# Row sums as four wide products, and token copies shared by alternate banks and awaited by halves

## The reference

```python
# first stack: DEPTH = 2, 16 heads of 64, D_FF = 2816
for layer in range(2):
    h = h + 0.5 * swiglu(rmsnorm(h, g1[layer]), ...)      # ffn0, ffn2
    hn = rmsnorm(h, gm[layer])
    h = h + (mixer_a(hn, ...) if layer == 0 else mixer_b(hn, ...))   # attention a, attention b
    h = h + 0.5 * swiglu(rmsnorm(h, g2[layer]), ...)      # ffn1, ffn3
    if layer == 0: shared = shared_kv(h, kv_norm, kv_w)   # keys and values of mixer_b
x = rmsnorm(h, final_norm)
# second stack: cs = silu(c), one vector of 1024
mod = cs @ ada_w[l] + ada_b[l]         # 6 rows of 1024 a layer, and 2 rows for the shared K/V
h = x * (1 + sc_m) + sh_m
y = rwkv7_time_mix(h) if l == 0 else fox_layer(h, kv)
x = layer_norm(ALPHA * x + (1 + gt_m) * y)
y = hier_moe(x * (1 + sc_f) + sh_f)    # 32 experts, top 2
x = layer_norm(ALPHA * x + (1 + gt_f) * y)
```

## Time and profile before

| | |
|---|---|
| median of three runs | 2657.39 us (2653.95 to 2661.37) |
| span of the profiled execution | 2656.2 us (its whole time isn't recorded beside it) |
| mean granted TensorE clock | 0.961 of 2.4 GHz |
| TensorE waits for expert gate weights | 59.9 us in 55 waits |
| TensorE waits for expert up weights | 19.0 us in 28 waits |
| row products of `mod_sums` | 224 passes in seven groups, 6.9 us a group |
| HBM read | 687.85 MB, 259 GB/s over the span |

### The profile page before, as it was taken

How to read it: one execution, slowest core, us unless ns; L and a number is a source line. 1 busy time by engine, 2 the same in 40 slices (tenths; PEclk the granted TensorE clock), 3 DMA queues, 4 the chain that set the end, 5 groups by cost and what they waited for, 6 DMA issues and landing times. The chain is left out here.

```text
span 2656.2 us, 40656 instructions
## 1 busy us (share of the span) xinstructions
PE 2450.2 (92%) x16214; PEld 1713.2 (64%) x16214; DVE 1291.0 (49%) x2016; ACT 736.4 (28%) x1086; POOL 157.2 (6%) x250
## 2 busy tenths in 40 slices
PE   8999999999998899999998999899888899999896
PEld 7998789989997799944885343333367653343332
DVE  7864468746875576445564321222266552222223
ACT  4334443334334433312221111111033521111111
POOL 1100001000110010020240000000000000000000
PEclk9999889999999899989998999999998999999998
DMA  8865238754873175433004899999953159999996
GB/s 336 309 236 181 74 123 311 277 191 175 316 277 127 64 271 212 166 130 131 33 4 153 360 423 423 424 423 424 422 191 133 48 215 423 423 423 424 423 424 280
DMA packets 110172, 690.77 MB, mean 260 GB/s; under 512 B 15760, under 2 KB 17104, under 8 KB 35168
## 3 DMA queue, kind: packets, MB, share of 16 engines
q1 hardware_dynamic: 88720, 618.10, 59.0%
q0 software_dynamic: 20320, 70.85, 7.2%
q10 hardware_dynamic: 1008, 0.06, 0.0%
HBM read 687.85 MB, written 1.11 MB: 259 GB/s over the span
## 5 line engine op out<-in xcount | busy, mean ns | idle before, releaser
L737 PE MATMUL bank<-ring,B 128*64 128x512 f32 (+1 forms) x1728 | 548.1, 597 | 59.9 <-DMA ring<-in_moe_wgate 59.9
L2045 DVE TENSOR_TENSOR ring_r<-ring,B_r 128x2048 fp32r<-128x2048 f32 x184 | 417.8, 2289 | 273.1 <-ACT B_r L1592 272.9
L737 PE MATMUL bank<-B_r 128*128 128x512 f32 (+1 forms) x1992 | 534.0, 353 | 13.8 <-DVE B_r L2382 6.0
L1592 ACT ACTIVATE B_r<-ring 128x2048 fp32r<-128x2048 f32 x184 | 347.0, 1909 | 293.7 <-PE bank L737 290.6
L737 PEld LDWEIGHTS bank<-B_r 128*128 128x128 f32 x1992 | 344.9, 193 | 111.3 <-issue 50.7
L737 PE MATMUL bank<-xt_r,B_r 128*128 128x256 f32 x1408 | 399.8, 284 | 5.4 <-DVE xt_r L2026 2.5
L737 PE MATMUL bank<-xt_r,ring_r 128*128 128x256 f32 x1408 | 398.4, 283 | 0.0
L737 PEld LDWEIGHTS bank<-ring,B 128*64 128x64 f32 (+1 forms) x1728 | 183.9, 143 | 325.1 <-issue 315.4
L737 PE MATMUL bank<-B 64*64 64x64 f32 (+7 forms) x2528 | 244.8, 289 | 38.8 <-DMA rows<-in_moe_wup 19.0
L737 PEld LDWEIGHTS bank<-xt_r,B_r 128*128 128x128 f32 x1408 | 269.9, 192 | 8.0 <-issue 5.2
L737 PEld LDWEIGHTS bank<-xt_r,ring_r 128*128 128x128 f32 x1408 | 269.9, 192 | 0.0
(11 more groups left out here) (361 smaller groups left out, 2895.8 us busy)
## 6 DMA issues: line engine op xcount, KB each, us to landing
ring<-in_moe_wgate SPq DMA_DIRECT2D x128, 1024.0 KB, 23.4
rows<-in_moe_wup SPq DMA_DIRECT2D x64, 1024.0 KB, 24.8
wks<-in_moe_wdown SPq DMA_DIRECT2D x64, 1024.0 KB, 23.1
ring<-in_ffn_w_gate SPq DMA_DIRECT2D x44, 1024.0 KB, 4.9
ring<-in_ffn_w_up SPq DMA_DIRECT2D x44, 1024.0 KB, 7.4
ring<-in_ffn_w_down SPq DMA_DIRECT2D x44, 1024.0 KB, 7.4
wks<-in_ada_w POOLq DMA_DIRECT2D x72, 512.0 KB, 6.1
ring<-in_moe_wup SPq DMA_DIRECT2D x32, 1024.0 KB, 22.7
```

Source lines behind the costliest of these rows:

```text
L737: ins = pe.matmul(out, lhsT, rhs, start=start, stop=stop, skip_group_check=True)
L1592: act.activation(hi, ring[:, slot, :], ACT.Copy).then_inc(sp_hi, 1)
L2045: dve.tensor_tensor(ring_r[:, slot, :], ring[:, slot, :], f32(hi), ALU.subtract).then_inc(sp_lo, 1)
```

## The change

1. `mod_sums`: four products with the column of ones as the stationary operand and 512 columns of the accumulator as the moving one. Product j writes row 32j of bank 7. ScalarE copies 97 rows of 512 columns, and the DMA takes every 32nd.
2. Fillers (`FILLED`) ahead of the transposes of mix_a, kv, mix_b (3), mix_r (6), ffn1 and ffn3 (4), in bank 4.
3. ScalarE copies banks 0 and 2 of a set of transposes, VectorE banks 1 and 3. The consumer on TensorE waits for the first two banks, and for the last two only where it needs them (`copied`).
4. In the first slab of an ffn both gate products come before both up products, and the wait for ScalarE's copy of the row moves behind the first gate product.
5. VectorE's split of the first projection unit at mix_a, kv and mix_b is cut in two halves, one before and one after the norm; at ffn1 and ffn3 the up split moves behind the low parts; at ffn2 VectorE copies tokens before it splits, and ScalarE copies them between its two splits.

```diff
+COPIED = {"qkv_a": "mix_a", "wo_a": "o_a", "kv_b": "kv", "q_b": "mix_b", "wo_b": "o_b", "kv_f": "kv_f", "wo_f": "o_f"}
+FILLED = {"mix_a": 3, "kv": 3, "mix_b": 3, "mix_r": 6, "ffn1": 4, "ffn3": 4}
...
-                for c in range(MODW // P):
-                    mm(bank[7][:, c:c + 1], mod_acc[r % 2].rearrange("p (m c) -> p c m", m=P)[:, c, :], cst("upto", TB, SEQ)[:, 0, SEQ - 1:SEQ],
-                       signal=mod_pe if c == MODW // P - 1 else None)
+                for j in range(MODW // BANK):
+                    mm(bank[7][32 * j:32 * j + 1, :], cst("upto", TB, SEQ)[:, 0, SEQ - 1:SEQ], mod_acc[r % 2][:, j * BANK:(j + 1) * BANK],
+                       signal=mod_pe if j == MODW // BANK - 1 else None)
...
+                if name in FILLED:
+                    stay_busy(4, FILLED[name])
...
-                        pe.wait_ge(tr_act if b < 2 else tr_dve, 2 * (n - 1) + b % 2 + 1)
+                        pe.wait_ge(tr_dve if b % 2 else tr_act, 2 * (n - 1) + b // 2 + 1)
...
+            def copied(name, c):
+                pe.wait_ge(tr_act, 2 * TRANS_AT[name] + 1 + c)
+                pe.wait_ge(tr_dve, 2 * TRANS_AT[name] + 1 + c)
...
             def first_gate(n, out, hi, w):
                 for k in range(KC):
+                    if k % 4 == 0:
+                        copied(f"ffn{n}", k // 4)
...
+                order = [(0, gate), (1, gate), (0, up), (1, up)] if s == 0 else [(0, gate), (0, up), (1, gate), (1, up)]
+                for c, (w, hi, o) in order:
...
             def ffn(n):
                 transposes(f"ffn{n}")
-                transposed(f"ffn{n}")
-                if f"ffn{n}" in MODS:
-                    pe.wait_ge(mod_take, MODS.index(f"ffn{n}") + 1)
...
# ScalarE
-                for b in range(2):
+                for b in (0, 2):
...
-                act.activation(mod_acc[r % 2][:, 0:MODW // P], bank[7][:, 0:MODW // P], ACT.Copy).then_inc(mod_take, 1)
+                act.activation(mod_acc[r % 2][0:97, 0:BANK], bank[7][0:97, :], ACT.Copy).then_inc(mod_take, 1)
...
-            ffn_first()
+            split(hi_gate(0))
             transposes("ffn2", xt_r, "ffn1_1")
+            split(hi_up(0))
...
# VectorE
-                for b in (2, 3):
+                for b in (1, 3):
...
+            def split_around(n, hi, between):
+                slot, _, _ = cur.take()
+                dve.wait_ge(sp_hi, SPLIT_AT[n] + 1)
+                a, b = slice(0, D), slice(D, 2 * D)
+                dve.tensor_tensor(ring_r[:, slot, a], ring[:, slot, a], f32(hi[:, a]), ALU.subtract)
+                between()
+                dve.tensor_tensor(ring_r[:, slot, b], ring[:, slot, b], f32(hi[:, b]), ALU.subtract).then_inc(sp_lo, 1)
...
-            normalise(1, "mix_a")
-            split("qkv_a", 0, hi_proj(0))
+            split_around("qkv_a", hi_proj(0), lambda: normalise(1, "mix_a"))
...
-            split(1, 1, hi_up(0))
             transposes("ffn1", xt_r, "ffn2_0")
             operand_lo("ffn1", "ffn2_0")
+            split(1, 1, hi_up(0))
...
-            ffn_first(2)
             transposes("ffn2", xt_r, "ffn1_1")
+            split(2, 0, hi_gate(0))
             operand_lo("ffn2", "ffn1_1")
+            split(2, 1, hi_up(0))
```

More of the change, by code:

```diff
@@ L792, in transposed, with project @@
                 pe.wait_ge(tr_dve, 2 * TRANS_AT[name] + 2)
-            def project(name, lhs, halves=TB):
+            def copied(name, c):
+                pe.wait_ge(tr_act, 2 * TRANS_AT[name] + 1 + c)
+                pe.wait_ge(tr_dve, 2 * TRANS_AT[name] + 1 + c)
+            def project(name, lhs, halves=TB, of=None):
                 first = PROJ_AT[name]
@@ L800, in project @@
                     for u in range(2):
+                        if of and b == first:
+                            copied(of, u)
                         s = unit()
@@ L821, in project_split @@
                         if b == first and u == 0:
+                            if name in COPIED:
+                                copied(COPIED[name], 0)
                             for h in range(TB):
@@ L834, in project_split @@
                             pe.wait_ge(xs_lo, 2 * SPLIT_NO[name] + 2)
+                            if name in COPIED:
+                                copied(COPIED[name], 1)
                             continue
@@ L876, in gate_up @@
                 split(n, gate_unit(s), i)
-                for c in range(2):
+                gate, up = (wg, hg, 0), (wu, hu, SEQ)
+                order = [(0, gate), (1, gate), (0, up), (1, up)] if s == 0 else [(0, gate), (0, up), (1, gate), (1, up)]
+                for c, (w, hi, o) in order:
                     q = 2 * (NSLAB * n + s) + c
-                    if q >= 4:
+                    if w is wg and q >= 4:
                         pe.wait_ge(ff_h, q - 3 if i is None else i * 4 + (q - 3))
[L881 to L893, removed]
+                    if w is wu and c == 0:
+                        split(n, gate_unit(s) + 1, i)
+                    if s == 0 and c == 0 and w is wg:
+                        first_gate(n, bank[4 + q % 4][:, 0:SEQ], hi, w)
+                        if f"ffn{n}" in MODS:
+                            pe.wait_ge(mod_take, MODS.index(f"ffn{n}") + 1)
+                        continue
+                    for k in range(KC):
+                        sig = None
+                        if k == KC - 1:
+                            sig = ff_gu if w is wu else w_free if c else None
+                        t = slice(c * P, (c + 1) * P)
+                        three(bank[4 + q % 4][:, o:o + SEQ], hi[:, k, t], w[:, k, t], xt_r[:, k, :], x_lo(k),
+                              k == 0, k == KC - 1, sig)
                 owed[0] += 1
@@ L944, in attention @@
                         r = i
+                        if r % 4 == 0:
+                            copied(("k_a", "q_b", "q_f")[n], r // 4)
                         if g + r >= 2:
@@ L1129, in moe @@
                     for k in range(KC):
+                        if t == 0 and k % 4 == 0:
+                            copied(f"moe{l}", k // 4)
                         mm(bank[t][:, 0:N_RT], xt[:, k, t * P:(t + 1) * P], rt_w[:, k, :], k == 0, k == KC - 1,
@@ L1407, in _ @@
             transposes("mix_a")
-            transposed("mix_a")
             project_split("qkv_a")
@@ L1411, in _ @@
             transposes("k_a")
-            transposed("k_a")
             wait_taken(pe, PROJ_AT["qkv_a"] + 5)
@@ L1415, in _ @@
             transposes("o_a")
-            transposed("o_a")
             project_split("wo_a")
@@ L1423, in _ @@
             transposes("mix_b")
-            transposed("mix_b")
             project_split("q_b")
@@ L1427, in _ @@
             transposes("q_b")
-            transposed("q_b")
             attention(1, QT, fm(B[2]), V)
             transposes("o_b")
-            transposed("o_b")
             project_split("wo_b")
@@ L1455, in _ @@
             transposes("y_r")
-            transposed("y_r")
-            project("wo_r", tokens_of(xt))
+            project("wo_r", tokens_of(xt), of="y_r")
             moe(0)
@@ L1461, in _ @@
             transposes("kv_f")
-            transposed("kv_f")
             project_split("kv_f")
@@ L1484, in _ @@
             transposes("q_f")
-            transposed("q_f")
             attention(2, QT, KT, fV, bias=True)
             transposes("o_f")
-            transposed("o_f")
             project_split("wo_f", hi_out)
@@ L2480, in _ @@
             normalise(2, "ffn1")
-            split(1, 1, hi_up(0))
             transposes("ffn1", xt_r, "ffn2_0")
             operand_lo("ffn1", "ffn2_0")
+            split(1, 1, hi_up(0))
             ffn(1)
-            normalise(3, "kv")
-            split("kv_b", 0, hi_proj(0))
+            split_around("kv_b", hi_proj(0), lambda: normalise(3, "kv"))
             transposes("kv", xt_r, "kv")
@@ L2490, in _ @@
             dve.engine_nop().then_inc(tr_src, 1)
-            ffn_first(2)
             transposes("ffn2", xt_r, "ffn1_1")
+            split(2, 0, hi_gate(0))
             operand_lo("ffn2", "ffn1_1")
+            split(2, 1, hi_up(0))
             ffn(2)
-            normalise(4, "mix_b")
-            split("q_b", 0, hi_proj(0))
+            split_around("q_b", hi_proj(0), lambda: normalise(4, "mix_b"))
             transposes("mix_b", xt_r, "mix_1")
@@ L2512, in _ @@
             normalise(5, "ffn3")
-            split(3, 1, hi_up(0))
             transposes("ffn3", xt_r, "ffn2_1")
             operand_lo("ffn3", "ffn2_1")
+            split(3, 1, hi_up(0))
             ffn(3)
```

4 lines of the change are left out of this document (1 added, 3 removed).

## The result

The kernel after takes 2621.70 us (median of four runs, 2618.45 to 2624.67) against 2657.38 us for the kernel before, measured beside it: ratio 0.9865, 95% interval 0.9847 to 0.9883, 35.7 us. The forecast was 2618 and the range 2606 to 2637. The experiments show that the time came out near the forecast by errors that cancel, and that some 25 us more lay beside the change.

What follows compares the result with a forecast made beforehand. TensorE bounds the trunk and weight DMA the expert layers, so trunk savings move everything behind them. Stage-border gains sum to 39.3 us: 2657.4 - 39.3 = 2618 us, range 2606 to 2637.

Steps and rivals of the forecast that it cites:

- The products: Per modulation row, 32 one-column passes (6.88 us) go and 4 products of 2 passes come, taking 2.1 us.
- TensorE takes passes in order: Row products: two passes of one product share their place, only neighbouring products overlap; five steps of 0.43, 2.1 us.
- side by side: Rival, chance 0.15: the four row products run together in two steps, 0.9 us; 2613 us in all.
- Fillers buy the clock: Ahead of transposes, fillers stand in idle or freed time (3 take 2.6 us) and what they buy is the clock.
- the clock falls all the same: Rival, chance 0.20: cold transposes at six stages and slow first passes at five cost some 16 us; 2634 us.
- slower: Rival, chance 0.03: row products and fillers ahead of mix_a, kv, mix_b, mix_r meet a low clock; 2678 us.
- The clock: Sign: granted clock 1.00 at 210 to 220; at ffn2 5.0 us taken for a clock possibly low part of the time.
- border terms: Gains forecast at borders of trunk stages, such as 5.6 us at mix_a, 5.2 at mix_b and 8.1 at ffn3.
- Copies by halves start early and then wait at the second unit for VectorE: Projections start about 1 us earlier, but the second unit starts 6.5 us behind the transposes, waiting 0.7 to 0.9 us.
- ScalarE's row copy and DMA cost nothing: The 512-column row copy (about 0.6 us) lies beside transposes and costs nothing; without that cover, 0.4 us a row.
- New orders: At ffn0 the second gate product fills a wait, 1.4 us; at ffn2 VectorE copies before its splits, within 5.0 us.
- Attentions and kv_f at zero: No gain or loss forecast inside the attentions; at kv_f 0, because VectorE's split ends the wait either way.

Runs made afterwards that it cites:

- second profile of after: The kernel after run once more, unchanged: 2619.03 us, span 2617.3 against 2623.0 in the first profile.

## Why the prediction came out right

By its own steps:

- *The products*: 8 passes for 32, right; "TensorE takes passes in order", five steps, 2.1 us, is the step that failed. It is two steps, 0.97 us, at all seven places. The rival "side by side" had the mechanism, and the Trainium skill ("TensorE: Matmul & The Clock Gate", Part 3) had the rule (about 4 ns a tile): here the four first passes start within 21 ns, 7 a tile, and the four second passes 0.43 us behind them. The two passes of one product do not hold up those of another group. The rival's extra gain shows in part: q_a 6.6 for 5.4. At mix_a a small slip of the forecast hides in it too: the second unit of before started at 223.47, not 223.2.
- *Fillers buy the clock*: right in kind. They are worth 7 us, not the 16 that the rival "the clock falls all the same" put on a low clock, because short products alone keep most of it. That they hide in idle time is right only behind the wide products; behind the narrow ones they stand on the path at half clock. That is the "slower" rival's mechanism, seen in a kernel in which the products themselves take the 6.9 us. There it cost 1.0 to 2.4 us at each of four borders, where the rival had 5.1 and 9.6; the kernel is 9.5 us slower than before, and in its profile the larger part of the loss lies in the attentions and from kv_f to q_f.
- *The clock*: 1.00 at mix_a, ffn1, mix_b and ffn3, right; ffn2 kept 3.4 us of low clock, as allowed for. With it the border terms hold to 1.2 us each, but for the stretch from mix_r to the router, 5.7 us for 1.4: its low clock went from 31.4 to 14.2 us. Whether the six fillers did that is open: of three kernels with the wide products and without the six two took 321 us there and one 314; the eight profiles with both took 312 to 319, after 316.
- *Copies by halves start early and then wait at the second unit for VectorE*: right in kind. The second unit waits 0.21 us at mix_a and 0.55 at kv and mix_b, where 0.7 to 0.9 was forecast; it starts 6.6 to 6.8 us behind the transposes' end, for 6.5. That ScalarE's row copy and DMA cost nothing was wrong by 0.7 us at the first unit of mix_a, which the second unit would have waited anyway.
- *New orders*: 3 us by the median, against the forecast's share at ffn0 and ffn2; right in place. At kv and ffn2, which the table takes together, the products alone gave 5.4 us and the orders 3.3.
- *Attentions and kv_f at zero*: wrong. The prediction moved their start and asked nothing of their clock. The waits at the three entrances grew from 2.99, 3.08 and 2.81 us to 4.36, 4.50 and 4.22, and the low clock in the attentions from 22.5 to 38.3 us. With kv_f and the rest that is 12.4 us given back, against 6.6 more than forecast at the borders. With this loss foreseen the same working would have said about 2630, with only the borders right about 2612. In the second profile of after the two are 6.4 us given back and 6.3 more than forecast. So that the time fell 4 us from the forecast is in part luck: two errors met in the middle.

The first attention came 14.5 us earlier (12 forecast), the first router 40.4 us earlier, and the expert layers kept it.

## What to carry to other kernels

Sum partitions with the ones as the stationary operand and the data moving, one result row for each column group: 32 passes became eight that take the time of two. Read the granted clock of every stage behind an idle stretch before pricing it at zero: TensorE at half clock looks exactly as busy, and moving a split out of the way, which took 3.3 to 3.6 us of wait out of the start of each of three attentions, was worth 26 us. Fillers pay only where TensorE would otherwise wait; price them at half clock when something slow stands before them.

## What the runs showed of the hardware

- Each column group works off its own passes, 0.43 us each for 512 float32 columns, whatever stands between them in the program. Products in different groups start about 7 ns apart.
- Where the clock falls is in part fixed by the kernel and in part not: one kernel, two executions, 151 and 137 us of low clock up to the end of the last expert layer, and spans 5.7 us apart.
- A wait of TensorE of 2.8 to 4.5 us at an attention's entrance went with a fall of the clock in 26 of 26 cases; with waits of at most 1.9 us there was no fall from there on in 15 of 16.
- The issue of a DMA with four partitions as source took ScalarE's queue 1.06 us at mix_a and 0.49 to 0.52 at the six other places, and held its next copy at mix_a; in before, with 128 partitions as source, it took 0.33 or 0.34.
